# A 31-tap depthwise convolution: from two to six of eight channel chunks on TensorE, as a two-phase form, with the groups around it reordered

## The reference

```python
u = h @ w_pw1 + b_pw1                       # 1024 -> 2048
a, gate = jnp.split(u, 2, axis=-1)
u = a * jax.nn.sigmoid(gate)                # the gated product, 1024 wide
u = lax.conv_general_dilated(               # depthwise: each channel by itself,
    u, w_dw[:, None, :].astype(u.dtype),    # 31 taps, causal (30 zeros in front)
    window_strides=(1,), padding=[(CONV_WIDTH - 1, 0)],
    dimension_numbers=("NWC", "WIO", "NWC"),
    feature_group_count=D_MODEL) + b_dw
u = jax.nn.silu(layernorm(u, ln_g, ln_b))
return u @ w_pw2 + b_pw2
```

## Time and profile before

| what | value |
|---|---|
| time of three runs | 2835.68, 2840.2, 2842.85 us; median 2840.2 us |
| span of the profiled execution | 2830.3 us (its own total is not given; the median is 9.9 us above the span) |
| PE busy | 2713.4 us, 96% |
| DVE busy | 1178.8 us, 42% |
| ACT busy | 972.5 us, 34% |
| POOL busy | 1232.2 us, 44% |
| HBM | 94 GB/s over the span |

### The profile page before, as it was taken

One profiled execution on the slowest core, in us unless ns is written; L12 is line 12 of the kernel. 1 busy time (PEld: TensorE's weight loads), 2 busy tenths in 40 slices (PEclk: granted clock), 3 DMA queues, 4 the chain that ended last, 5 costly groups with the idle time before them and its releaser, 6 DMA issues.

```text
span 2830.3 us, 31426 instructions
## 1 busy us (share of the span) xinstructions
PE 2713.4 (96%) x12328; PEld 2243.1 (79%) x12328; DVE 1178.8 (42%) x1415; ACT 972.5 (34%) x1317; POOL 1232.2 (44%) x590
## 2 busy tenths in 40 slices
PE   7788599999999999999999999999999999999998
PEld 6677488888888877888888888888888877888887
DVE  6999744411234366434112373421214249321213
ACT  4224334322233355343222332332223248422223
POOL 3564444444444334444444444444444435444442
PEclk9898799999999988999999999999999989999999
DMA  4541222232232211412323333323333311322331
GB/s 154 175 145 38 85 88 66 89 105 97 96 97 84 90 38 40 154 60 90 104 97 97 97 97 97 97 90 98 104 97 97 94 59 49 98 96 90 104 97 60
DMA packets 169854, 262.42 MB, mean 93 GB/s; under 512 B 16370, under 2 KB 78250, under 8 KB 168698
## 3 DMA queue, kind: packets, MB, share of 16 engines
q1 hardware_dynamic: 159690, 235.22, 25.9%
q10 hardware_dynamic: 10032, 25.38, 2.7%
HBM read 254.17 MB, written 11.61 MB: 94 GB/s over the span
## 4 chain that ended last, share of the span: by engine, by line
PE 87%; issue 5%; DVE 4%; ACT 2%; DVEq 1%; DMA 0%; ACTq 0%; POOL 0%
PE ps L756 79%; PE ps L876 3%; PE ps L909 2%; DVE conv L1578 1%; PE ps L895 1%; ACT prob L1268 1%; PE ps L880 1%; ACT pt_hi L1283 1%; DVE prob L1679 0%; DVEq L1574 0%; PE ps L686 0%; DMA xnat<-in_x 0%; DVE t L1418 0%; DVE small L1689 0%; ACT q_hi L1288 0%
## 5 line engine op out<-in xcount | busy, mean ns | idle before, releaser
L629 POOL TENSOR_TENSOR w_lo<-stage,w_hi 128x1024 fp32r<-128x1024 f32 x444 | 1101.0, 2487 | 1327.3 <-ACT w_hi L984 1327.3
L984 ACT ACTIVATE w_hi<-stage 128x1024 fp32r<-128x1024 f32 x444 | 462.0, 1054 | 1128.5 <-PE ps L756 1118.1
L756 PE MATMUL ps<-h_hi,w_hi 128*128 128x512 f32 x1920 | 753.8, 393 | 4.0 <-issue 3.2
L756 PE MATMUL ps<-h_lo,w_hi 128*128 128x512 f32 x1920 | 749.0, 390 | 0.0
L756 PE MATMUL ps<-h_hi,w_lo 128*128 128x512 f32 x1920 | 748.7, 390 | 0.0
L756 PEld LDWEIGHTS ps<-h_hi,w_hi 128*128 128x128 f32 x1920 | 361.5, 188 | 81.6 <-issue 6.0
L756 PEld LDWEIGHTS ps<-h_lo,w_hi 128*128 128x128 f32 x1920 | 361.2, 188 | 77.0 <-issue 2.7
L756 PEld LDWEIGHTS ps<-h_hi,w_lo 128*128 128x128 f32 x1920 | 361.3, 188 | 75.1
L756 PE MATMUL ps<-mid_hi,w_hi 128*128 128x512 f32 x992 | 387.5, 391 | 6.5 <-DVE mid_lo L1341 6.5
L1421 DVE TENSOR_TENSOR t<-ps,rstd 128x1024 f32<-128x1024 f32 x104 | 122.5, 1219 | 649.8 <-PE ps L756 648.6
L756 PE MATMUL ps<-mid_hi,w_lo 128*128 128x512 f32 x992 | 387.2, 390 | 0.0
(11 more groups left out here) (223 smaller groups left out, 2910.2 us busy)
## 6 DMA issues: line engine op xcount, KB each, us to landing
stage<-in_ff_w SPq DMA_DIRECT2D x256, 256.0 KB, 2.9
stage<-in_ffn_w_gate SPq DMA_DIRECT2D x88, 256.0 KB, 2.8
stage<-in_ffn_w_up SPq DMA_DIRECT2D x88, 256.0 KB, 3.0
stage<-in_ffn_w_down SPq DMA_DIRECT2D x88, 256.0 KB, 2.9
stage<-in_conv_pw_w SPq DMA_DIRECT2D x48, 256.0 KB, 3.1
stage<-in_conv_w_in SPq DMA_DIRECT2D x48, 256.0 KB, 2.9
stage<-in_attn_w_qkv SPq DMA_DIRECT2D x48, 256.0 KB, 3.0
stage<-in_mem_wk SPq DMA_DIRECT2D x32, 256.0 KB, 3.2
```

Source lines behind the costliest of these rows:

```text
L629: pool.tensor_tensor(w_lo[:, slot], stage[:, slot], w_hi[:, slot].bitcast(F32), ALU.subtract).then_inc(tile_lo, 1)
L756: last = pe.matmul(ps[:, base + n, 0:width], lhs, mov, start=k == 0 and m == 0, stop=k == 2 * tiles - 1 and m == 2)
L984: act.activation(w_hi[:, slot], stage[:, slot], ACT.Copy).then_inc(tile_hi, 1)
```

## The change

Six of the eight chunks are made on PE, and only chunks 0 and 1 by taps on DVE (62 instead of 186). The form on PE is another one: 64 channels fill the partitions twice, once with the even tokens and once with the odd ones (`u2_hi`, `u2_lo`). One matmul of 256 columns (token pairs) then adds two taps for both phases; 31 taps need 16 shifts. A chunk is two halves of 64 channels: 2 x 16 x 3 passes = 96 matmuls of 256 columns. The weights of a shift have four blocks of 64 x 64 diagonals; they are built in rounds of four shifts, four rounds per half, over three buffers, the high parts now on DVE (not on ACT), the low parts on POOL. The tables of taps that they need are made by `tap_tables` near the start. `conv_out` writes a chunk out of PSUM with four instructions. G1, G2 and G3 are now of the kind `glu_split`: their product is written by eight small instructions into the two-phase layout `u2` and split into parts.

The core of the diff:

```diff
+    def conv_pair(pair, u_parts, between, after_turn=False):
+        do("lo_ahead", {}, 2)
+        for a in range(2):
+            for half in range(2):
+                do("conv_half", {}, 2 * pair + a, half, u_parts, after_turn)
+                taps(between)
+            do("conv_out", dict(psum_read=1), 2 * pair + a)
+        b.parity ^= 1
...
     do("mem_rows", MEM_ROWS)
+    do("tap_tables", TAP_TABLES)
     normed("glu", "pw1", "h")
     mem_turn(1)
-    taps(10)
-    groups("glu", "pw1", "h", g=1, after_turn=True)
+    taps(5)
+    keys0, keys1, values0, values1 = mem_kv_groups(1)
+    groups("glu_split", "pw1", "h", g=1, after_turn=True)
+    u_parts = b.count["part_lo"]
     do("skew", {})
-    for n, group in zip((4, 6, 6, 6), mem_kv_groups(1)):
-        taps(n)
-        group()
+    taps(3)
+    keys0()
+    taps(4)
+    keys1()
+    conv_pair(0, u_parts, 1)
+    taps(3)
+    groups("glu_split", "pw1", "h", g=2, lo_done=2)
+    u_parts = b.count["part_lo"]
+    taps(3)
+    values0()
+    taps(3)
+    values1()
     mem_turn(0)
-    taps(12)
-    groups("glu", "pw1", "h", g=2, after_turn=True)
     do("keys_out", {})
-    do("diag_hi_first", {})
-    taps(13)
-    groups("glu_split", "pw1", "h", g=3, settled=True)
-    do("diag_lo_first", {})
+    conv_pair(1, u_parts, 1, after_turn=True)
+    taps(DVE_PAIRS * TAPS)
+    groups("glu_split", "pw1", "h", g=3, settled=True, lo_done=2)
+    u_parts = b.count["part_lo"]
     keys0, keys1, values0, values1 = mem_kv_groups(0)
-    taps(4)
     keys0()
-    taps(6)
-    keys1()
-    taps(DVE_PAIRS * TAPS)
-    do("conv_pe", CONV_PE)
-    b.parity ^= 1
+    do("conv_sum", CONV_SUM)
+    conv_pair(2, u_parts, 0)
+    keys1(lo_done=2)
     do("ln_centred", LN_CENTRED)
...
+        def conv_half(q, half, u_parts, after_turn):      # PE
+            bank = 4 * b.parity + q % 2
+            for m in range(HALF_ROUNDS):
+                r = (2 * q + half) * HALF_ROUNDS + m
+                pe.wait_ge(diag_hi, r + 1)
+                pe.wait_ge(diag_lo, r + 1)
+                for i in range(ROUND):
+                    k = ROUND * m + i
+                    for p, (part, u) in enumerate(((0, u2_hi), (0, u2_lo), (1, u2_hi))):
+                        last = pe.matmul(ps[:, bank, PAIRS_T * half:PAIRS_T * (half + 1)], diag[:, r % DIAGS, part, i, :],
+                                         u[:, q % 2, half, k:k + PAIRS_T], start=k == 0 and p == 0,
+                                         stop=k == SHIFTS - 1 and p == 2)
                 last.then_inc(diag_used, 1)
...
+        def conv_half(q, half, u_parts, after_turn):      # DVE; POOL has the same with tap_lo
+            for m in range(HALF_ROUNDS):
+                r = (2 * q + half) * HALF_ROUNDS + m
+                if r >= DIAGS:
+                    dve.wait_ge(diag_used, r - DIAGS + 1)
+                dve.tensor_tensor(half_tiles(diag[:, r % DIAGS, 0]), twin[:, :].unsqueeze(1).broadcast_to([P, 2 * ROUND, HP]),
+                                  tap_t[:, q, half, 2 * ROUND * m:2 * ROUND * (m + 1)].unsqueeze(2)
+                                  .broadcast_to([P, 2 * ROUND, HP]), ALU.mult).then_inc(diag_hi, 1)
...
+        def conv_out(q):
+            c = 2 * DVE_PAIRS + q
+            dve.wait_ge(diag_used, 2 * HALF_ROUNDS * (q + 1))
...
+                    for half in range(2):
+                        rows = slice(half * HP, (half + 1) * HP)
+                        for ph in range(2):
+                            last = dve.scalar_tensor_tensor(out=u2[ph * HP:(ph + 1) * HP, a, half, :],
+                                                            in0=phase(t[rows, 2 + a, :], ph), in1=phase(t[rows, a, :], ph),
+                                                            scalar=bias_c[rows, :], op0=ALU.add, op1=ALU.mult)
```

More of the change, by code:

```diff
@@ L618, in _, with group, lo_ahead @@
                            base=0, pattern=[[-1, P]], channel_multiplier=1).then_inc(consts, 1)
-        def group(kind, src, g, rhs, dst, fresh, tiles, after=None, **_):
-            for j in range(2 if after else 0, tiles):
+        def group(kind, src, g, rhs, dst, fresh, tiles, after=None, lo_done=0, **_):
+            for j in range(2 if after else lo_done, tiles):
+                tile(j)
+        def lo_ahead(n):
+            for j in range(n):
                 tile(j)
@@ L833, in ln_centred @@
             pe.wait_ge(psum_read, b.at("psum_read"))
-            for c in range(2 * DVE_PAIRS, DC):
+            for c in range(6, DC):
                 last = pe.matmul(ps[:, 4 * b.parity + 3, :], ones[:, :], conv[:, c, :], start=False, stop=c == DC - 1)
@@ new lines, in conv_out @@
+        def conv_out(q):
+            c = 2 * DVE_PAIRS + q
+            dve.wait_ge(diag_used, 2 * HALF_ROUNDS * (q + 1))
+            for half in range(2):
+                rows = slice(half * HP, (half + 1) * HP)
+                for odd in range(2):
+                    frm = slice((1 - odd) * HP, (2 - odd) * HP)
+                    last = dve.tensor_scalar(phase(conv[rows, c, :], odd),
+                                             ps[frm, 4 * b.parity + q % 2, PAIRS_T * half:PAIRS_T * (half + 1)],
+                                             column(VECTORS["conv_dw_b"] + c)[rows, :], None, ALU.add)
+            last.then_inc(psum_read, 1)
@@ L1586, in conv_pe, with conv_sum @@
+        def conv_sum():
+            dve.wait_ge(step, b.at("step"))
+            dve.wait_ge(psum_read, b.at("psum_read"))
+            for c in range(1, 6):
                 dve.tensor_tensor(acc[:, :], conv[:, 0, :] if c == 1 else acc[:, :], conv[:, c, :],
```

142 lines of the change are left out of this document (73 added, 69 removed).

## The result

The changed kernel takes 2872.6 us (median of four runs, 2868.05 to 2880.25), the kernel before 2841.33 us beside it. The ratio is 1.0118 with a 95% interval from 1.0097 to 1.0140. I had forecast 2858, slower with a chance of 0.70. The direction was right and the time lies in the range, but the slowdown is about twice what I gave. The profiled execution has a span of 2864.6 us, 34.3 above the 2830.3 of before; I had 17.3. So 17.0 us are to be found.

The account below looks back on a forecast made before the run. VectorE was taken to bound the 252.50 us convolution stretch. Added TensorE work 26.9, waits -14.3, ahead +7 and behind -2.3 made +17.3 us; with the 2830.3 span and 9.9 around it, 2858 us, range 2832 to 2882.

Parts of the forecast that it names:

- (a): K0 of layer 1 waits for G1's reads, sigmoid, small products and parts, with slow clock after; 10.9 us.
- (b): K1 of layer 1 waits for K0's parts, with slow clock after; 3.9 us.
- (d): Mid-pair, VectorE writes out the first chunk and builds a round before TensorE has weights; three times 2.7, 8.1 us.
- (j): The third pair waits for K0's drain, the five additions of conv_sum and a round; 7.1 us.
- (g): The fourth tile of the group behind G2 and G3 comes late, split only after u2_hi; 5.6 us.
- (e): Slow clock behind six gaps, at the start and middle of each pair, 1.7 us each; 10.2 us.
- (f): Late diagonal rounds inside the pairs, 1.5, and two taps in the middle of a chunk, 2.7; 4.2 us.
- (h): M0 waits for the six taps queued behind V0's drain; 1.5 us.
- The tables: Ahead of the stretch, tap_tables on VectorE delays TensorE's sum: 6 us and 1 for the clock, +7 us.
- VectorE is ahead at every handover: Rival, 12%: VectorE is free when a group ends, each handover costs its low end, 28.6 us in all; 2823 us.
- The clock holds: Rival, 18%: gaps of 3 us don't slow TensorE, so the clock terms go; +3 us, 2843, no change.
- The rounds don't balance: Rival, 10%: VectorE and GpSimd wait out each other's whole time, 48 rounds pace 0.21 us slower; 2868 and above.

Follow-up runs that it names:

- x_taps: Changed kernel with the two blocks of six taps around V0 and V1 moved behind the second pair; 2869.67 us, 1.0118 of the kernel before.
- x_tables: Changed kernel with the tables of taps made behind mem_turn of layer 1; 2866.75 us, 1.0099 of the kernel before.
- x_all: Changed kernel with tables, taps, K0/K1 waits, chunk outputs, first rounds, fourth tile and chunk sum all reordered together; 2826.13 us, 0.9961 of the kernel before.

## Why the prediction was off, point by point

**What bounds the kernel, and the direction: right.** Only the stretch ahead of pw2 changed, the work on TensorE rose as given (each chunk of the convolution at full clock takes 11.7 us, 96 x 0.122), and the new waits stand in the places that I listed.

**Terms within 1.7 us.** (Slow clock is what a group takes above its time at full clock, gaps left out.) (a) 9.25 us idle and 1.4 of slow clock, 10.6 for 10.9. (b) 2.92 and 1.5, 4.4 for 3.9. (c) 3.67 for 3.5. (d) 3.41, 3.12 and 2.80, 9.3 for 8.1. (i) 4.18 for 4.1. (j) 8.49 for 7.1: VectorE's second `km_lo` waited out a `w_lo` (the two took 2.42 us). In (g), K0 of layer 0: 2.79 and 1.5, 4.3 for 2.6. Together 4.8 more than given.

**(e) and (f), too high.** The six chunks took 13.19, 13.22, 14.05, 13.84, 13.88 and 11.74 us, 79.9 where full clock makes 6 x 11.68 = 70.1: 9.8 for slow clock and late rounds together, for which I gave 14.4. That is 4.6 less, and the two groups nearly cancel (+0.2).

**The step that failed is (h) with V0's and V1's part of (g).** I gave 3.0 us for V0's fourth tile, nothing for V1's, and in (h) "M0 waits for the six taps queued behind V0's drain. **1.5.**" Measured are 3.25, 2.04 and 4.47 us idle, and 5.0 of slow clock (V0 and V1 took 26.9 us where full clock makes 21.9): 14.8 for 4.5, **10.3 of the 17.0 us**. I had costed the taps as undisturbed ones, 4.0 us for six. The price stood in my own rows: four `w_lo` beside taps take 11.10 us, 2.8 for each pair of tap and `w_lo`. I used it for VectorE's sum over the stretch, and not at the one place where TensorE waits for the taps' end. x_taps shows it: without those twelve taps 9.56 us go at just this place, for which (h) had 1.5. The rest is V0's own gap, 3.25 us idle and 1.9 of slow clock behind it (x_taps, where V0 and V1 take 23.8 us beside the gap) for the 3.0 that I gave it: I had put a price on the gap and none on the clock behind it.

**The tables, 9.1 for 7.** My bounds were 3 and 9 for the instructions alone. x_tables shows what the upper one consists of: GpSimd's `w_lo` beside them. **LN:** from its first sum to pw2 40.9 us (338.44 to 379.31) for 41.6 of before, -0.8 where I gave -2.3 (and the sum starts at 338.44 where I gave 324). **Behind pw2** 1.2 more. **Work:** ten blocks of 96 matmuls of 256 columns take 11.68 us each, not 11.52, 1.6 in all. With the main miss that is 10.3 + 0.2 + 2.1 + 1.5 + 1.2 + 1.6 = 16.9 of the 17.0. The median lies 14.6 above the forecast and not 17.0, since it stands 8.0 us above the profiled span where I had 9.9, and by 0.5 of rounding.

**The rivals.** "VectorE is ahead at every handover": no. The stretch has 71 us of waits and slow clock beside its 206 of work (61.19 to 338.44), and even in x_all, with the order made for it, 41 (54.34 to 301.46). That is above the 37 of this rival and under the 46.5 at which the change pays, and there the sign did turn. "The clock holds": not behind the gaps at the pairs' starts, and once behind a gap of 2.80 us (last section). "The rounds don't balance": they do. In the third pair a round takes 1.44 us, TensorE's own pace, with 0.7 us of idle time on VectorE in each.

**The port.** In all these places an instruction of VectorE that reads SBUF and meets one of GpSimd ends only after it: 2.85 us for a tap, 2.61 for a product of 0.48, 2.47 for a cast of 0.36, while two copies out of PSUM take their 0.68 us each in x_all, from 261.20 on, beside a low diagonal that runs from 260.70 to 262.18. The Trainium skill ("SBUF — State Buffer", section "SBUF: two separate sides") says that a VectorE operation with two SBUF inputs, or one in a two-port mode, and one of GpSimd can't both hold the shared pair of ports: whichever starts first has it for its whole instruction, and the other is fully blocked. I had weighed this rule against a mean of 0.83 us per round and kept the mean. The stretched instructions agree with the rule; in a row of such meetings a tap and a low diagonal come every 1.45 us (0.69 + 1.04 would be 1.73), and a tap and a `w_lo` every 2.8 (0.67 + 2.40 would be 3.07), so a meeting costs 0.3 us less than the sum.

It is not always VectorE that gives way. The first taps in the changed kernel are a row of eight, and one `w_lo` falls into it:

```profile
67.13 5.38 DVE L1601 SCALAR_TENSOR_TENSOR conv<-u_pad,vec,conv 128x512 f32<-128x512 f32 x8
```

```profile
68.19 6.59 POOL L668 TENSOR_TENSOR w_lo<-stage,w_hi 128x1024 fp32r<-128x1024 f32 x1 [3.03 <-ACT w_hi L1015]
```

The taps keep their 0.67 us each, and `w_lo` takes 6.59 instead of 2.4. The case that I had put up against the rule in the prediction is the same: beside the 24 undisturbed taps of the kernel before one `w_lo` runs from 163.40 for 14.28 us and ends 2.3 after the last tap, so it was held up for the whole row. That is no sign against a lock, as I had read it. Nor does the order of starts settle who waits: at 201.77 another `w_lo` starts beside a row of taps that began at 201.39, and there they alternate. What decides it no run here shows.
